# Turning x without its norm factor, in four transfers, with the factor applied to the first projection's sums

## Chip, cores, metric

One core of one Trainium2 chip. The metric is the device time of one launch in microseconds (us), the median over several runs. In the profile PE is the tensor engine's matmuls, PEld its weight loads, DVE the vector engine, ACT the scalar engine, SP the sync engine; a "q" behind a name (ACTq, SPq) is that engine's issuing of DMAs.

## What is computed

Two transformer blocks, one after the other, on one sequence of 256 tokens of width 2048, in float32. The change touches the very beginning of the first block, the RMS norm of the input and the projection that follows:

```python
def rmsnorm(x, g):
    y = xf * lax.rsqrt(jnp.mean(xf * xf, axis=-1, keepdims=True) + EPS)
    return (y * g.astype(jnp.float32)).astype(x.dtype)

h = rmsnorm(x, norm_mix[l])          # x: (1, 256, 2048)
z = h @ w_in[l]                      # w_in: (2048, 9472)
hq, hf, hi, hgate, aq, ak, av, g_hg, g_at = jnp.split(z, offsets, axis=-1)
```

The parts of `z` feed a gated linear recurrence (hq, hf, hi, hgate), a windowed attention (aq, ak, av; queries and keys are normed again per head) and two gates; then follow an output projection, a feed-forward part of width 8192, and a second block of similar shape.

## The kernel before

**Weights stream.** All weight matrices are cut into panels of 512 input features by 512 columns (1 MB), which SP loads into four slots of `raw`. A panel is two halves. For each half ACT writes its rounded high part to `wh` (`feed`, L1082) and DVE the remainder to `wl` (`feed`, L1782); both keep four halves ahead of PE at most, because `wh` and `wl` have four slots (`half_used`). PE makes of a half 4 tiles x (2 matmuls of `wh` with 512 columns, 2 of `wl` with 256): function `step`, L484 and L488. The 512 columns are the 256 tokens' high part and their low part, both in `hs`. Four panels (8 halves) are one step, which gives 512 columns of `z`; the first layer has 11 of them, numbered from 0 (two of them, for hi, run with the operands exchanged, function `across`).

**End of a step.** ACT copies the second half of each accumulator to `te` (`copy_halves`), DVE adds it to the first half and writes `z` (`total`, L1823), and signals `tile_summed`. A step may reuse its PSUM banks once the step before last is summed.

**The beginning.** x comes in two transfers of 128 tokens each, on SP's queue, ahead of the first panel. ACT squares and sums each (L1205), takes the root of both (L1211), DVE inverts it and multiplies x with it in four pieces of 512 features (`first_normed`, L1968, result `xn`). PE transposes `xn` (`first_turn(j)`, L618: 4 transposes for 256 features, j = 0 to 7), ACT scales the result by `norm_mix` and writes the high part (`first_high(j)`, L1218), DVE writes the low part (`first_low(j)`, L1976, signal `hs_lo`). Half h of step 0 needs `first_low(h)`. Turns 0 to 3 stand ahead of step 0, turns 4 to 7 behind its halves 0 to 3, and `vectors_turn`, which transposes small parameter vectors, behind half 5.

**Order.** Each engine runs its own list of instructions in the order in which the code writes it; semaphores link the lists. So a wait in ACT's list holds up all that stands behind it, its later `feed`s too.

**Two other places.** Queries are normed in step 10 (the last, 2 tiles wide): `pair_squares` on ACT waits until step 9 (z index 36 to 39) is fully summed, squares it into `psq` (L1185), and PE's `query_sums` (L593, behind half 3 of step 10) adds the squares up. In the feed-forward part the kernel already applies a norm factor behind a projection: it puts the factors on a diagonal (`turned_r`, L2299), spreads them over the partitions with a matmul by ones (`factors_across`, L546), copies them to `rstd` and multiplies the sums.

Of the kernel before, what the change touches and what calls it, by code (L numbers as in the profile page):

```python
# [23 lines left out]
P = 128  # L24
# [96 lines left out]
def build(nc, x, norm_mix, w_in, lb_logits, hg_norm, q_norm, k_norm, sinks, w_hg_out, w_at_out,  # L121
# [9 lines left out]
    with ctx:  # L131
# [136 lines left out]
        vectors_loaded, small_loaded, x_loaded = sem("vectors_loaded"), sem("small_loaded"), [sem("x_loaded0"), sem("x_loaded1")]  # L268
# [13 lines left out]
        def _(sp):  # L282
# [13 lines left out]
            for t in range(2):  # L296
                sp.dma_start(xin[:, t, :], x[0, t * P:(t + 1) * P, :]).then_inc(x_loaded[t], 16)
# [169 lines left out]
        def _(pe):  # L467
# [73 lines left out]
            def factors_across():  # L541

                pe.wait_ge(sem("row_diagonal"), 2)
# [67 lines left out]
            def first_turn(j):  # L611

                pe.wait_ge(sem("x_normed"), 2 * (j // 2) + 2)
                if j >= 4:
                    pe.wait_ge(sem("hs_lo"), 2 * (j - 4) + 2)
                for a in range(2):
                    for t in range(2):
                        mm = nc.tensor.transpose(ps[:, 4 + j % 4, a * T + t * P:a * T + (t + 1) * P],  # L618
                                                 xn[:, t, (2 * j + a) * P:(2 * j + a + 1) * P], ident[:])
# [5 lines left out]

            def vectors_turn():
                pe.wait_ge(vectors_loaded, 16 * N_VECTORS)
# [217 lines left out]
            def ffn_chunk(c):  # L845
                t = LF1.step + 4 * c
                for s in range(4):
# [4 lines left out]
                    if (c, s) == (0, 1):  # L852
                        pe.wait_ge(sem("rooted"), 1)
# [219 lines left out]
        def _(act):  # L1073
            def feed(h, dp):
# [4 lines left out]
                if q == 0:  # L1079
# [123 lines left out]
            for t in range(2):  # L1203
                act.wait_ge(x_loaded[t], 16)
                nc.scalar.activation(xn[:, t, :], xin[:, t, :], ACT.Square, accum_out=x_sum[:, t:t + 1]  # L1205
                                     ).then_inc(sem("x_squared"), 1)
                if t == 0:
                    act.wait_ge(sem("vectors_turned"), 1)
                    nc.scalar.activation(cols[:, 0:ND], ps[:, 3, 0:ND], ACT.Copy).then_inc(sem("cols_ready"), 1)
            act.wait_ge(sem("x_squared"), 2)  # L1210
            nc.scalar.activation(x_root, x_sum, ACT.Sqrt, bias=eps, scale=1.0 / D).then_inc(sem("x_rooted"), 1)  # L1211
# [56 lines left out]
            def hg_values(d):  # L1268

                for i in range(2):  # L1270
                    if i == 0:
                        act.wait_ge(across_done, d + 1)
                    else:
                        act.wait_ge(half_used, 8 * (5 + d) + 4)
                    nc.scalar.activation(z[:, Z_HI + 4 * d:Z_HI + 4 * d + 4, i * P:(i + 1) * P],
                                         ps[:, 4 * d + i, :].rearrange("p (h c) -> p h c", h=4), ACT.Copy
                                         ).then_inc(sem("v_ready"), 1)

            for d in range(2):
# [122 lines left out]
            def gates_out(s):  # L1402
# [3 lines left out]
                for i in range(2):  # L1406
# [4 lines left out]
                    nc.scalar.activation(gs[:, i, :], ps[:, (2, 0)[s % 2] + i, :], ACT.Copy  # L1411
# [49 lines left out]
            def hidden(c):  # L1461

                for s in range(4):
                    p, t = LF1.panel + 4 * s, LF1.step + 4 * c + s
                    for h in range(8):
                        feed(2 * p + h + 4, 32 * c)
                        if (c, s) == (0, 0):
# [5 lines left out]
                            if h == 5:  # L1473
                                act.wait_ge(sem("norm_summed"), 1)
# [291 lines left out]
        def _(dve):  # L1766
# [58 lines left out]

            def summed(t, dt, n):
# [135 lines left out]
            dve.wait_ge(sem("x_rooted"), 1)  # L1962
            link(nc.vector.reciprocal(x_root, x_root))

            def first_normed(q):
                c = slice(512 * q, 512 * q + 512)
                for t in range(2):
                    nc.vector.tensor_scalar(xn[:, t, c], xin[:, t, c], x_root[:, t:t + 1], None, ALU.mult  # L1968
                                            ).then_inc(sem("x_normed"), 1)
# [716 lines left out]
```

## Time and profile before

| what | value |
|---|---|
| median of 3 runs | 2529.32 us (2529.02 to 2529.37) |
| span of the profiled execution, first to last instruction | 2527.6 us |
| what lies around the span, against the median | 1.7 us |
| PE busy | 2493.5 us, 99% of the span |
| DVE busy | 1779.8 us, 70% |
| ACT busy | 1229.6 us, 49% |
| first matmul of step 0 | 15.73 us after the span's start |

The profiled execution's own time is not given apart from its span; the runs agree within 0.35 us, so span plus 1.7 us is taken for it. Busy shares are means over the whole span; what one place costs is read from the timeline around it. PE is busy almost always, so each microsecond in which it waits or does extra work counts nearly in full, and work of DVE or ACT counts only where PE is made to wait for it.

### The profile page before, as it was taken

The page shows a single profiled execution, that of the slowest core. Times are in us where ns is not written, and L with a number is a line of the kernel's source. Part 1 is how long each engine was busy: PE and PEld are TensorE (multiplying, and loading weights), DVE is VectorE, ACT ScalarE, POOL GpSimd, SP SyncE. Part 2 cuts the span into 40 slices and gives each one's busy share as a digit, 9 for nine tenths or more (in the row PEclk, how much of TensorE's full clock was granted, in tenths as well). Part 3 has the DMA queues.
Part 4 walks back from the last instruction along what each step waited for, and adds up shares of the span by engine and source line. Part 5 has one row for each costly group of instructions (what it writes and reads, how often), then busy time and mean ns, then how long its engine had stood idle before and what let it go on. Part 6 is the DMA issues. An engine that isn't in the chain of part 4 may idle for free.

```text
span 2527.6 us, 33151 instructions
## 1 busy us (share of the span) xinstructions
PE 2493.5 (99%) x13297; PEld 2116.8 (84%) x13297; DVE 1779.8 (70%) x2426; ACT 1229.6 (49%) x1801; POOL 0.2 (0%) x4
## 2 busy tenths in 40 slices
PE   8999999999999999999999999999899999999998
PEld 7888877888888888888887899978788888888887
DVE  6556657577788788788888767676866556665555
ACT  6456446454544444443444444565544444443453
POOL 0000000000000000000000000000000000000000
PEclk9999999999999999999999999999999999999999
DMA  7555445888778879879788545456577667657554
GB/s 260 192 186 180 153 146 179 300 294 280 264 263 302 283 268 317 283 261 327 261 281 297 180 160 169 143 166 215 177 239 236 221 212 234 226 190 214 186 183 134
DMA packets 324537, 572.53 MB, mean 227 GB/s; under 512 B 28649, under 2 KB 124215, under 8 KB 323487
## 3 DMA queue, kind: packets, MB, share of 16 engines
q1 hardware_dynamic: 277484, 449.44, 53.8%
q10 hardware_dynamic: 46899, 120.97, 13.7%
q8 instruction: 105, 1.72, 0.3%
q14 instruction: 49, 0.40, 0.0%
HBM read 560.63 MB, written 8.60 MB: 225 GB/s over the span
## 4 chain that ended last, share of the span: by engine, by line
PE 94%; DVE 3%; ACT 1%; DMA 1%; issue 1%; ACTq 0%; DVEq 0%; SPq 0%
PE ps L484 28%; PE ps L513 14%; PE ps L488 14%; PE ps L514 14%; PE ps L515 14%; PE ps L1002 2%; PE ps L1003 2%; PE ps L1004 2%; DVE wl L1782 1%; DMA gate_at<-gate_spill 1%; ACT wh L1082 1%; PE ps L888 1%; PE ps L593 0%; PE ps L687 0%; DVE ts L1906 0%
## 5 line engine op out<-in xcount | busy, mean ns | idle before, releaser
L1782 DVE TENSOR_TENSOR wl<-raw,wh 128x1024 fp32r<-128x1024 f32 x856 | 1041.0, 1223 | 710.1 <-ACT wh L1082 707.4
L1082 ACT ACTIVATE wh<-raw 128x1024 fp32r<-128x1024 f32 x856 | 899.4, 1058 | 1083.9 <-PE ps L515 505.3
L484 PE MATMUL ps<-hs,wh 128*128 128x512 f32 (+1 forms) x3152 | 994.6, 397 | 1.1 <-DVE hs L1854 0.7
L488 PEld LDWEIGHTS ps<-hs,wl 128*128 128x128 f32 (+1 forms) x3152 | 592.9, 188 | 141.2
L488 PE MATMUL ps<-hs,wl 128*128 128x256 f32 (+1 forms) x3152 | 620.7, 278 | 0.0
L484 PEld LDWEIGHTS ps<-hs,wh 128*128 128x128 f32 (+1 forms) x3152 | 481.9, 189 | 3.2 <-issue 1.5
L513 PE MATMUL ps<-wh,ff 128*128 128x512 f32 x864 | 336.2, 389 | 0.0
L514 PE MATMUL ps<-wl,ff 128*128 128x512 f32 x864 | 336.1, 389 | 0.0
L515 PE MATMUL ps<-wh,ff 128*128 128x512 f32 x864 | 336.1, 389 | 0.0
L513 PE MATMUL ps<-wh,hs 128*128 128x512 f32 x640 | 257.2, 402 | 0.0
L515 PE MATMUL ps<-wh,hs 128*128 128x512 f32 x640 | 249.8, 390 | 0.0
L514 PE MATMUL ps<-wl,hs 128*128 128x512 f32 x640 | 249.6, 390 | 0.0
L515 PEld LDWEIGHTS ps<-wh,ff 128*128 128x128 f32 x864 | 162.2, 188 | 33.7
L513 PEld LDWEIGHTS ps<-wh,ff 128*128 128x128 f32 x864 | 162.2, 188 | 33.5
L514 PEld LDWEIGHTS ps<-wl,ff 128*128 128x128 f32 x864 | 162.2, 188 | 33.1
L513 PEld LDWEIGHTS ps<-wh,hs 128*128 128x128 f32 x640 | 120.2, 188 | 30.1 <-issue 5.5
L515 PEld LDWEIGHTS ps<-wh,hs 128*128 128x128 f32 x640 | 120.1, 188 | 26.4
L514 PEld LDWEIGHTS ps<-wl,hs 128*128 128x128 f32 x640 | 120.4, 188 | 22.9
L1800 DVE SCALAR_TENSOR_TENSOR ada_acc<-ada_more,sm_cols,ada_acc 128x1024 f32<-128x1024 f32 x96 | 122.7, 1278 | 0.0
L1002 PE MATMUL ps<-hs,wh 128*128 128x256 f32 x384 | 111.0, 289 | 0.0
L1003 PE MATMUL ps<-hs,wl 128*128 128x256 f32 x384 | 108.6, 283 | 0.0
L1004 PE MATMUL ps<-hs,wh 128*128 128x256 f32 x384 | 108.5, 283 | 0.0
(296 smaller groups left out, 1782.7 us busy)
## 6 DMA issues: line engine op xcount, KB each, us to landing
raw<-w_in SPq DMA_DIRECT2D x112, 1024.0 KB
raw<-w_down SPq DMA_DIRECT2D x108, 1024.0 KB
raw<-w_up SPq DMA_DIRECT2D x64, 1024.0 KB
ada_w<-w_ada ACTq DMA_DIRECT2D x96, 512.0 KB, 5.5
ada_more<-w_ada ACTq DMA_DIRECT2D x96, 512.0 KB, 6.4
raw<-w_gate SPq DMA_DIRECT2D x88, 512.0 KB
raw<-w_up SPq DMA_DIRECT2D x88, 512.0 KB
raw<-w_out SPq DMA_DIRECT2D x16, 1024.0 KB
```

Source lines behind the costliest of these rows:

```text
L484: nc.tensor.matmul(ps[0:m, b, :], wh[:, slot, w0:w0 + m], rhs(n, k), start=k == 0, stop=False)
L488: mm = nc.tensor.matmul(ps[0:m, b, 0:T], wl[:, slot, w0:w0 + m], rhs(n, k)[:, 0:T], start=False, stop=k == 4 * panels - 1)
L513: nc.tensor.matmul(sums, hi, wh[:, slot, w], start=k == 0, stop=False)
L514: nc.tensor.matmul(sums, hi, wl[:, slot, w], start=False, stop=False)
L515: mm = nc.tensor.matmul(sums, lo, wh[:, slot, w], start=False, stop=k == 2 * last + 1)
L888: mm = nc.tensor.matmul(ps[:, 4 + i % 4, QT[qt]], z[half(i), Z_IQ + i // 2, qt * P:(qt + 1) * P], z[half(i), Z_IK, 0:KEYS[qt]], start=True ...
L1002: nc.tensor.matmul(sums, wh[:, slot, w0:w0 + m], hs[:, k, 0:T], start=k == 0, stop=False)
L1003: nc.tensor.matmul(sums, wl[:, slot, w0:w0 + m], hs[:, k, 0:T], start=False, stop=False)
L1004: mm = nc.tensor.matmul(sums, wh[:, slot, w0:w0 + m], hs[:, k, T:2 * T], start=False, stop=k == ND - 1)
L1082: nc.scalar.activation(wh[:, h % WH_SLOTS, :], raw[:, slot, HALF * q:HALF * (q + 1)], ACT.Copy).then_inc(wh_ready, 1)
L1782: nc.vector.tensor_tensor(wl[:, h % WH_SLOTS, :], raw[:, slot, HALF * q:HALF * (q + 1)], wh[:, h % WH_SLOTS, :], ALU.subtract).then_inc(wl ...
L1800: ins = nc.vector.scalar_tensor_tensor(out=ada_acc[:], in0=ada_ring[k % 4], scalar=csil[:, k:k + 1], in1=ada_acc[:], op0=ALU.mult, op1=ALU ...
```

## The change

- x's two transfers on SP's queue become four on ACT's queue, each of 512 features of all 256 tokens, so that `xin[p, t, d]` is token 128 t + p, as before. SP's queue begins with the first weight panel, which is cut into two transfers with a semaphore each.
- PE transposes x itself (`xin`), not `xn`; DVE's `first_normed` is gone. Turns 0 and 1 stand ahead of step 0, turns 2 to 7 behind its halves 0 to 5.
- The squares of x and their root stand in ACT's list behind the `feed`s at halves 4 and 5 of step 0. DVE inverts behind its `feed` at half 5 and writes the two diagonals; PE's new `factors_of_x` stands behind half 6, ahead of `vectors_turn`, which moved there from half 5; ACT copies the factors to `rstd` ahead of the parameter columns; step 1 waits for that.
- `total` becomes `totals_of_x` for every step of the first layer that writes `z` in this layout: the 4 sums as before, then 4 multiplies by `rstd`, and only these signal `tile_summed`. Where tokens lie on partitions (hi, gates) the factor is the `scale` of a copy that ACT makes anyway.

```diff
-            for t in range(2):
-                sp.dma_start(xin[:, t, :], x[0, t * P:(t + 1) * P, :]).then_inc(x_loaded[t], 16)
...
+                        if (i, s, k) == (0, 0, 0):
+                            sp.dma_start(slots[:, 0, 0:2, :], win[:, 0:2, 0:512]).then_inc(sem("first_loaded"), 16)
+                            sp.dma_start(slots[:, 0, 2:4, :], win[:, 2:4, 0:512]).then_inc(raw_loaded[0], PANEL_INC)
+                            continue
...
             def first_turn(j):
-                pe.wait_ge(sem("x_normed"), 2 * (j // 2) + 2)
+                pe.wait_ge(x_loaded[j // 2], 16)
...
+            def factors_of_x():
+                pe.wait_ge(sem("row_diagonal"), 2)
+                pe.wait_ge(sem("hs_lo"), 12)
+                for i in range(2):
+                    mm = nc.tensor.matmul(ps[:, 5, i * P:(i + 1) * P], ones[:], turned_r[:, i, :], start=True, stop=True)
+                mm.then_inc(sem("norm_summed"), 1)
...
-            for j in range(4):
-                first_turn(j)
+            first_turn(0)
+            first_turn(1)
             step(0, 0, 0, 0, FULL, from_hs, split=(sem("hs_lo"), 0),
-                 after=dict([(h, first_turn_after(4 + h)) for h in range(4)] + [(5, vectors_turn)]))
+                 after=dict([(h, first_turn_after(2 + h)) for h in range(6)] + [(6, vectors_turn)]))
             pe.wait_ge(sem("hs_lo"), ND)
             pe.wait_ge(sem("cols_ready"), 3)
+            pe.wait_ge(sem("rooted"), 1)
...
+            x_tokens = x[0].rearrange("(t p) d -> p t d", t=2)
+            for q in range(4):
+                act.dma_start(xin[:, :, 512 * q:512 * q + 512], x_tokens[:, :, 512 * q:512 * q + 512]
+                              ).then_inc(x_loaded[q], 16)
...
+            def x_square(t):
+                for q in range(4):
+                    act.wait_ge(x_loaded[q], 16)
                 nc.scalar.activation(xn[:, t, :], xin[:, t, :], ACT.Square, accum_out=x_sum[:, t:t + 1]
                                      ).then_inc(sem("x_squared"), 1)
+                if t:
+                    act.wait_ge(sem("x_squared"), 2)
+                    nc.scalar.activation(x_root, x_sum, ACT.Sqrt, bias=eps, scale=1.0 / D).then_inc(sem("x_rooted"), 1)
...
                     if s == 0 and h < 4:
                         first_high(4 + h)
+                    if s == 0 and h in (4, 5):
+                        x_square(h - 4)
                     if (s, h) == (0, 6):
+                        act.wait_ge(sem("norm_summed"), 1)
+                        nc.scalar.activation(rstd[:, 0, :], ps[:, 5, 0:T], ACT.Copy).then_inc(sem("rooted"), 1)
...
+            def totals_of_x(t, tiles):
+                for n, dst in enumerate(tiles):
+                    dve.wait_ge(half_copied, 4 * t + n + 1)
+                    nc.vector.tensor_tensor(dst, ps[:, bank(t, n), 0:T], te[:, n, :], ALU.add).then_inc(sem("dve_part"), 1)
+                if t == 0:
+                    dve.wait_ge(sem("rooted"), 1)
+                for n, dst in enumerate(tiles):
+                    dve.wait_ge(sem("dve_part"), 4 * t + n + 1)
+                    nc.vector.tensor_tensor(dst, dst, rstd[:, 0, :], ALU.mult
+                                            ).then_inc(tile_summed, 1 if n < len(tiles) - 1 else 4 - n)
...
+            def x_invert():
+                dve.wait_ge(sem("x_rooted"), 1)
+                nc.vector.reciprocal(x_root, x_root).then_inc(sem("x_rooted"), 1)
+                dve.wait_ge(sem("x_rooted"), 2)
+                for i in range(2):
+                    nc.vector.tensor_scalar(turned_r[:, i, :], ident[:], x_root[:, i:i + 1], None, ALU.mult
+                                            ).then_inc(sem("row_diagonal"), 1)
```

ACT's list before, from the end of its DMA issues to the first two halves (L1205 squares, L1211 root, L1082 `feed`, L1218 `first_high`):

```order
L1202 ACTIVATE sm_cols<-sm_cols 128x1 [waits consts_set]
L1205 ACTIVATE xn,sm_cols<-xin 128x2048 [waits x_loaded0]
L1209 ACTIVATE cols<-ps 128x16 [waits vectors_turned]
L1205 ACTIVATE xn,sm_cols<-xin 128x2048 [waits x_loaded1]
L1211 ACTIVATE sm_cols<-sm_cols 128x2 [waits x_squared]
L1082 ACTIVATE wh<-raw 128x1024 [waits half_used,raw_loaded0,cols_ready]
L1218 ACTIVATE hs<-ps,cols 128x256 [waits xn_turned]
```

ACT's list of the change, from the `feed` of half 7 on, which is where the squares (L1228) and the root (L1232) stand now; L1096 is `feed`, L1239 `first_high(7)`, L1272 the copy of the factors:

```order
L1096 ACTIVATE wh<-raw 128x1024 [waits half_used]
L1239 ACTIVATE hs<-ps,cols 128x256 [waits xn_turned]
L1239 ACTIVATE hs<-ps,cols 128x256
L1096 ACTIVATE wh<-raw 128x1024 [waits half_used,raw_loaded0]
L1228 ACTIVATE xn,sm_cols<-xin 128x2048 [waits x_loaded2,x_loaded3,x_loaded1,x_loaded0]
L1096 ACTIVATE wh<-raw 128x1024 [waits half_used]
L1228 ACTIVATE xn,sm_cols<-xin 128x2048 [waits x_loaded2,x_loaded3,x_loaded1,x_loaded0]
L1232 ACTIVATE sm_cols<-sm_cols 128x2 [waits x_squared]
L1096 ACTIVATE wh<-raw 128x1024 [waits half_used,raw_loaded1]
L1272 ACTIVATE rstd<-ps 128x256 [waits norm_summed]
```

So both squares and the root moved from ahead of the first `feed` to behind the `feed`s of halves 8 and 9, and those stand behind `first_high(7)`.

PE's list of the change, the end of half 6 and the beginning of half 7 of step 0; L633 is `factors_of_x`, L640 and L641 `vectors_turn`:

```order
L486 MATMUL ps<-hs,wh 128x512 x2
L490 MATMUL ps<-hs,wl 128x256 x2
L633 MATMUL ps<-turned_r,ones 128x128 [waits hs_lo,row_diagonal]
L633 MATMUL ps<-turned_r,ones 128x128
L640 MATMUL ps<-ident,rows_88 128x96 [waits hs_lo,vectors_loaded]
L641 MATMUL ps<-ident,rows_89 128x124
L486 MATMUL ps<-hs,wh 128x512 [waits wl_ready,hs_lo]
```

Before, nothing stood between halves 6 and 7; the two transposes of the vectors stood a half earlier, and there was no wait for a diagonal.

DVE's list of the change around the end of step 0; L1856 are the sums, L1861 the multiplies, L2006 the diagonals:

```order
L1808 TENSOR_TENSOR wl<-raw,wh 128x1024 [waits wh_ready] x2
L2003 RECIPROCAL sm_cols<-sm_cols 128x2 [waits x_rooted]
L2006 TENSOR_SCALAR turned_r<-ident,sm_cols 128x128 [waits x_rooted]
L2006 TENSOR_SCALAR turned_r<-ident,sm_cols 128x128
L1808 TENSOR_TENSOR wl<-raw,wh 128x1024 [waits wh_ready] x2
L1856 TENSOR_TENSOR z<-ps,te 128x256 [waits half_copied] x4
L1861 TENSOR_TENSOR z<-z,rstd 128x256 [waits dve_part,rooted]
L1861 TENSOR_TENSOR z<-z,rstd 128x256 [waits dve_part] x3
```

Before, the four sums (L1823) were followed by the next `feed` at once.

## Rows read from the trace of the kernel before

**Rows 1.** The page: busy time, and the chain that ended last

```profile
PE 2493.5 (99%) x13297; PEld 2116.8 (84%) x13297; DVE 1779.8 (70%) x2426; ACT 1229.6 (49%) x1801; POOL 0.2 (0%) x4
PE 94%; DVE 3%; ACT 1%; DMA 1%; issue 1%; ACTq 0%; DVEq 0%; SPq 0%
```

**Rows 2.** Timeline to step 0: start, duration, engine, line, operands [idle before]

```profile
8.90 1.91 ACT L1205 ACTIVATE xn<-xin 128x2048 f32<-128x2048 f32 x1 [0.45 <-DMA xin<-x]
10.94 0.29 ACT L1211 ACTIVATE sm_cols<-sm_cols 128x2 f32<-128x2 f32 x1
11.68 1.06 ACT L1082 ACTIVATE wh<-raw 128x1024 fp32r<-128x1024 f32 x1 [0.45 <-DMA raw<-w_in]
12.40 3.67 PE L618 MATMUL ps<-ident,xn 128*128 128x128 f32 x16 [5.07 <-DVE xn L1968]
13.55 0.84 ACT L1218 ACTIVATE hs<-ps,cols 128x256 fp32r<-128x256 f32 x2 [0.81 <-PE ps L618]
15.73 0.94 PE L484 MATMUL ps<-hs,wh 128*128 128x512 f32 x2
```

**Rows 3.** DMAs: xin's times to landing, ident's median, one window (last: GB/s)

```profile
DMA to landing us min/median/max: 5.6/6.7/7.7
...
ident<-k_ident ACTq DMA_DIRECT2D x1, 64.0 KB, 5.4
...
8.00:10.00 2.00, 0.00 (x0) 0.00 (x0) 0.00 (x0) 1.55 (x4) 0.00 (x0) 1.00 1.04 406
```

**Rows 4.** Timeline, PE: first matmuls of halves 3, 4 and 7 and of step 1

```profile
26.25 0.71 PE L484 MATMUL ps<-hs,wh 128*128 128x512 f32 x2
...
29.50 0.71 PE L484 MATMUL ps<-hs,wh 128*128 128x512 f32 x2
...
38.17 0.62 PE L484 MATMUL ps<-hs,wh 128*128 128x512 f32 x2
...
40.96 0.62 PE L484 MATMUL ps<-hs,wh 128*128 128x512 f32 x2
```

**Rows 5.** Timeline, ACT: two feeds with one first_high between

```profile
15.94 1.08 ACT L1082 ACTIVATE wh<-raw 128x1024 fp32r<-128x1024 f32 x1
...
16.89 0.85 ACT L1218 ACTIVATE hs<-ps,cols 128x256 fp32r<-128x256 f32 x2
...
17.60 1.09 ACT L1082 ACTIVATE wh<-raw 128x1024 fp32r<-128x1024 f32 x1
```

**Rows 6.** Timeline of the feed-forward part: root, spread by ones, next half

```profile
685.43 0.29 ACT L1138 ACTIVATE sm_cols<-sm_cols 128x2 f32<-128x2 f32 x1 [1.02 <-DVE sm_cols L1880]
...
686.50 0.71 PE L546 MATMUL ps<-turned_r,ones 128*128 128x128 f32 x4 [0.42 <-DVE turned_r L2299]
...
686.97 0.70 PE L484 MATMUL ps<-hs,wh 128*128 128x512 f32 x2
```

**Rows 7.** Windows (PE busy and count first, clock third last) and PE's idle times

```profile
38.00:60.00 22.00, 22.00 (x128) 19.21 (x127) 15.61 (x32) 15.25 (x23) 0.00 (x0) 1.00 0.60 198
...
1381.19 1.23 PE L569 MATMUL ps<-ident,a_rows 128*128 128x128 f32 x6 [2.59 <-DVE a_rows L1896]
...
1380.00:1390.00 10.00, 7.93 (x32) 6.38 (x33) 9.01 (x21) 4.62 (x9) 0.00 (x0) 0.66 0.54 178
...
1384.00:1388.00 4.00, 4.00 (x13) 3.43 (x14) 3.94 (x9) 2.61 (x5) 0.00 (x0) 0.50 0.17 63
...
1779.85 1.11 PE L569 MATMUL ps<-ident,f_rows 128*128 128x128 f32 x4 [6.09 <-DVE f_rows L1896]
...
1775.00:1789.00 14.00, 7.61 (x29) 5.86 (x30) 13.11 (x30) 8.57 (x22) 0.00 (x0) 0.63 0.09 23
```

**Rows 8.** Timeline around the sums of step 9 and the queries' squares

```profile
242.97 1.41 DVE L1823 TENSOR_TENSOR z<-ps,te 128x256 f32<-128x256 f32 x4
...
244.65 1.17 ACT L1185 ACTIVATE psq<-z 128x512 f32<-128x512 f32 x2
...
248.28 1.90 PE L593 MATMUL ps<-psq,sel 128*20 128x256 f32 x8 [0.17 <-ACT psq L1185]
```

More of the change, by code:

```diff
@@ L267, in build @@
         ada_spilled, ada_back = sem("ada_spilled"), sem("ada_back")
-        vectors_loaded, small_loaded, x_loaded = sem("vectors_loaded"), sem("small_loaded"), [sem("x_loaded0"), sem("x_loaded1")]
+        vectors_loaded, small_loaded, x_loaded = sem("vectors_loaded"), sem("small_loaded"), [sem(f"x_loaded{q}") for q in range(4)]
         block = ctx.enter_context(nc.Block())
@@ L618, in first_turn @@
                         mm = nc.tensor.transpose(ps[:, 4 + j % 4, a * T + t * P:a * T + (t + 1) * P],
-                                                 xn[:, t, (2 * j + a) * P:(2 * j + a + 1) * P], ident[:])
+                                                 xin[:, t, (2 * j + a) * P:(2 * j + a + 1) * P], ident[:])
                 mm.then_inc(sem("xn_turned"), 1)
@@ L624, in first_turn_after @@
                 return lambda: first_turn(j)
+            def factors_of_x():
[4 more added lines that the diff above has]
+                mm.then_inc(sem("norm_summed"), 1)
             def vectors_turn():
+                factors_of_x()
                 pe.wait_ge(vectors_loaded, 16 * N_VECTORS)
@@ L1078, in feed @@
                 slot, q = (h // 2) % RAW_SLOTS, h % 2
-                if q == 0:
+                if h == 0:
+                    act.wait_ge(sem("first_loaded"), 16)
+                elif q == 0 or h == 1:
                     act.wait_ge(raw_loaded[slot], PANEL_INC * (h // 8 + 1) + PANEL_INC // 4 * dp)
@@ L1199, in _ @@
                           ).then_inc(sem("ident_loaded"), 16)
+            x_tokens = x[0].rearrange("(t p) d -> p t d", t=2)
+            for q in range(4):
+                act.dma_start(xin[:, :, 512 * q:512 * q + 512], x_tokens[:, :, 512 * q:512 * q + 512]
+                              ).then_inc(x_loaded[q], 16)
             act.wait_ge(sem("consts_set"), 3)
             nc.scalar.activation(m8[:, 1, 4:5], eps, ACT.Sqrt)
-            for t in range(2):
-                act.wait_ge(x_loaded[t], 16)
+            act.wait_ge(sem("vectors_turned"), 1)
+            nc.scalar.activation(cols[:, 0:ND], ps[:, 3, 0:ND], ACT.Copy).then_inc(sem("cols_ready"), 1)
+            def x_square(t):
+                for q in range(4):
+                    act.wait_ge(x_loaded[q], 16)
                 nc.scalar.activation(xn[:, t, :], xin[:, t, :], ACT.Square, accum_out=x_sum[:, t:t + 1]
                                      ).then_inc(sem("x_squared"), 1)
[L1207 to L1211, printed above, removed]
+                if t:
+                    act.wait_ge(sem("x_squared"), 2)
+                    nc.scalar.activation(x_root, x_sum, ACT.Sqrt, bias=eps, scale=1.0 / D).then_inc(sem("x_rooted"), 1)
             def first_high(j):
@@ L1275, in hg_values @@
                     nc.scalar.activation(z[:, Z_HI + 4 * d:Z_HI + 4 * d + 4, i * P:(i + 1) * P],
-                                         ps[:, 4 * d + i, :].rearrange("p (h c) -> p h c", h=4), ACT.Copy
-                                         ).then_inc(sem("v_ready"), 1)
+                                         ps[:, 4 * d + i, :].rearrange("p (h c) -> p h c", h=4), ACT.Copy,
+                                         scale=x_root[:, i:i + 1]).then_inc(sem("v_ready"), 1)
+            act.wait_ge(sem("x_rooted"), 2)
             for d in range(2):
@@ L1410, in gates_out @@
                         act.wait_ge(half_used, 2 * (LG.panel + 4 * s) + 12)
-                    nc.scalar.activation(gs[:, i, :], ps[:, (2, 0)[s % 2] + i, :], ACT.Copy
+                    nc.scalar.activation(gs[:, i, :], ps[:, (2, 0)[s % 2] + i, :], ACT.Copy, scale=x_root[:, i:i + 1]
                                          ).then_inc(sem("gate_copied"), 1)
@@ L1960, in _ @@
             nc.vector.memset(m8[:, 1, 0:2], 0.0).then_inc(ada_folded, 1)
[L1962 to L1969, printed above, removed]
+            def x_invert():
[5 more added lines that the diff above has]
+                                            ).then_inc(sem("row_diagonal"), 1)
             def first_low(j):
@@ L2038, in to_z @@
             def to_z(i, s, t):
-                for n in range(4):
-                    total(t, 2 * i, n, z[:, 8 * i + 4 * s + n, :])
+                totals_of_x(t + 2 * i, [z[:, 8 * i + 4 * s + n, :] for n in range(4)])
             for s in range(2):
@@ L2046, in _ @@
                         first_low(4 + h)
+                    if (s, h) == (0, 5):
+                        x_invert()
                     if (s, h) == (1, 0):
@@ L2127, in _ @@
                 if s < 10:
-                    for n in range(4):
-                        total(s - 2, 0, n, z[:, 4 * s + n, :])
+                    totals_of_x(s - 2, [z[:, 4 * s + n, :] for n in range(4)])
             def hg_mask(h):
```

21 lines of the change are left out of this document (7 added, 14 removed).

## The prediction

> **What bounds the kernel now.** I read the page first: PE is busy 99% of the span, and 94% of the chain that ended last is PE [rows 1]. So a part of the change counts as far as it moves PE's list, and the whole of it lies within the first 260 us. Next the timeline of the beginning. PE's first real work waits for a chain: x lands, ACT squares it twice (1.91 us each), takes the root by 11.23, DVE multiplies x, and PE can turn it at 12.40, after an idle time of 5.07 us put down to DVE; ACT's high part follows at 13.55 and step 0 starts at 15.73 [rows 2]. From there PE keeps its own pace: halves 3 and 4 start 3.25 us apart with a turn between them, half 7 and step 1 2.79 us apart without one [rows 4]. So a half is 2.79, a turn on PE 0.46, and step 0 lasts 25.23 us (15.73 to 40.96). Later feeds and sums of ACT and DVE lie beside that.
>
> **Term 1: the start.** Gone from the path are the squares, the root and DVE's multiplies. What starts the chain now is the landing of x's first quarter. To time it I fit the transfers of before: 2.1 MB of x and the small ones landed at 8.9 us, when ACT's second wait for x ended [rows 2] (5.6 to 7.7 us after their issue [rows 3]), and panel 0, 3.2 MB in all, at 11.68, when ACT's feed of half 0 stopped waiting for it [rows 2]. The rate was some 0.4 MB per us (406 GB/s in one window [rows 3]), which makes a landing 3.5 us plus bytes over 0.395. x's first quarter (0.52 MB) stands in ACT's queue behind ident and norm_mix, 0.07 MB; SP's queue is about 0.9 us ahead (0.36 MB), and then I let both queues have half the rate each: 0.36 + 2 x 0.6 = 1.56 MB, so 7.4 us. The two queues did share before: ident, 64 KB, took 5.4 us beside x [rows 3]. From a turn's start to ACT's high part was 1.15 us (12.40 to 13.55), from there to step 0 2.18 (13.55 to 15.73) [rows 2]. Step 0 starts at 7.4 + 1.15 + 2.18 = 10.7, and **5.0 us are won**. The first panel's first half (0.52 MB, in front of its queue) lands earlier than x's quarter, and the high parts of ACT need no more than one feed (1.06) ahead. Bounds: if the quarter had the whole rate, it would land at 5.0 and the start be 8.3, if ACT is through with its issues by then; if SP's first two panels' worth went ahead of it, (2.1 + 0.6)/0.395 + 3.5 = 10.3, start 13.6. I take 10.7, since the row of ident shows sharing. Panel 1 and x's later quarters land by the same rule at 13.2 and 10 to 15.5; they are wanted from 14 to 24, so I cost them at nothing, and about 1 us of delay each if the cover is short.
>
> The Trainium skill (DMA: Bandwidth & Descriptors, Queues, rings and completion order) has each DMA engine take turns between the queues that hold work, which is the half rate that the row of ident suggests; by that rule alone the start is again 10.7.
>
> **Term 2: work that moves onto PE's list.** Two of the four turns that stood ahead of step 0 now stand inside it, 2 x 0.46 = 0.9 us. The factors' two matmuls by ones cost 0.47, as in the feed-forward part (686.50 to 686.97 [rows 6]). `vectors_turn` only moves by a half. **1.4 us lost.**
>
> **Term 3: a hole in step 0.** This is what I think matters most. PE waits behind half 6 for the diagonal. Turn 7 now stands behind half 5, so ACT's `first_high(7)` waits for it, and in ACT's list the feed of half 8, the first square, the feed of half 9, the second square and the root all stand behind `first_high(7)`. Counted from the end of half 5 on PE: turn 7 and its signal 0.85 (an estimate between the 0.46 that a turn takes on PE and the 1.15 of a cold one), a high pair 0.71 (16.89 to 17.60), a feed 0.95 (15.94 to 16.89 [rows 5]), a square 1.91, a feed 0.95, a square up to the root's start 2.04 (8.90 to 10.94 [rows 2]), the root 0.29, then reciprocal, two diagonals and the signal to PE 0.78 (685.72 to 686.50 [rows 6]). The sum is 8.5 us. PE meanwhile has turn 7 and half 6, 3.25 us. **PE stands still for 5.2 us.** The feeds of halves 8 and 9 don't rescue it: they are needed only by step 1, but they are in the list. Nor is their panel late: its load waits for DVE's second feed and for SP's small transfers, as before. Bounds: 4.5 (0.3 less at the turn, less at the squares) and 6.5 (panel 4 late by 1.3). Step 1's new wait for `rstd` costs nothing: after the root ACT has one feed (0.95) and the copy of the factors, while PE runs half 7, 2.79 us; without this cover it would cost about 0.5.
>
> Step 0 then takes 8 x 2.79 for its halves, 6 x 0.46 for turns, 5.2 for the hole, 0.47 for the factors and 0.3 for the vectors' transposes (29.50 to 38.17 is 8.67, 3 halves and 0.3 [rows 4]): 31.1 us. Started at 10.7 it ends at 41.8, against 40.96 before: **the start's gain is used up, +0.8 us.** (The sum of the terms, -5.0 + 1.4 + 5.2, is 1.6; the other 0.8 is PE's stalls between the first halves before, when DVE's late multiplies of x held up turn 4: 25.23 is that much longer than 8 x 2.79 + 4 x 0.46 + 0.3.)
>
> **Term 4: the clock behind the hole.** In the trace PE's granted clock falls from 2.4 to 1.2 GHz at the two places in mid-kernel where PE had stood idle: 2.59 us before 1381.19, where the mean of ten us was 0.66, thus 6.8 us at the lower level; and 6.09 us before 1779.85, with 0.63 over 14 us, 10.4 us at the lower level. In 1384 to 1388, wholly at the lower level, PE started 13 matmuls in 4 us (3.25 per us), against 128 in 22 us (5.8 per us) at the full one [rows 7]: a stretch of dense matmuls loses 0.44 of its length. A hole of 5.2 us lies between these two. I let 1.8 of the 6.8 us fall into the hole and 5 on dense matmuls: **2.2 us lost**. Bounds: nothing, since the idle 5.07 us before 12.40 drew no lower level (step 0's first pair took 0.94 us), and 3.6 (8 us, from the longer case).
>
> The Trainium skill (TensorE: Matmul & The Clock Gate, Part 1) says that idleness brings the array to 1.2 GHz and activity releases it; by it the sum holds Term 4, without it the sum is that of the first rival. The same section calls the lower rate the default before any activity, and there the trace disagrees, as step 0 began at the full pace.
>
> **Term 5: the multiplies on DVE.** Each step of the first layer gets 4 multiplies 128x256, about as dear as the 4 sums (1.41 us for four [rows 8]). In steps 0 to 8 they are hidden: PE has four halves of cover (11 us), and DVE was busy for 15.61 of the 22 us of a step [rows 7]. Behind step 9 they are not. The squares of the queries start at 244.65, 0.3 us after the sums end (244.38) [rows 8]; now they wait for the multiplies, to 245.85, 1.2 us later. PE's `query_sums` is already held up there by these squares (idle 0.17 at 248.28 [rows 8]). Through two squares, two feeds (0.95 each) and the next two squares, PE is done with them at 251.5 instead of 250.18: **1.3 us lost**. Bounds 0.9, and 1.8 if the two multiplies behind step 10 also delay the next feed.
>
> **Nothing:** the scales in ACT's copies for hi and the gates (a Copy with a scale, as `first_high` is one already), and the renamed semaphores.
>
> **Sum.** 0.8 + 2.2 + 1.3 = 4.3 us over the profiled execution: span 2527.6 to 2531.9. With the 1.7 us around it that is, against the median, 2529.3 + 4.3 = 2533.6. A change of 0.2%, 5.1 us, is about what measurement can tell from none; so I forecast no change that can be told, on the slow side.
>
> **Rivals.**
> - *The same without the lower clock.* For it speaks the idle time ahead of 12.40; against it both idle times in mid-kernel. 0.8 + 1.3 = +2.1: 2531.4.
> - *x's first quarter is late.* It starts behind SP's panels instead of beside them, ACT's four issues taking long or the queue being served second. The start is 13.6 and not 10.7, +2.9 on everything: +7.2, 2536.5, slower. It decides from a landing 0.8 us later than I forecast. The shared rate before speaks against it, the many small descriptors of x in its new form for it. A low clock of 8 us, 0.8 + 3.6 + 1.3 = +5.7, 2535.0, ends on the same side.
> - *No hole.* ACT gets to the squares early enough, so that Terms 3 and 4 fall away: 0.8 - 5.2 + 1.3 = -3.1: 2526.2. ACT's list speaks against it, since `first_high(7)` stands ahead of the squares. Even so the gain stays under 0.2%.
>
> **Chances.** Forecast 0.47, no lower clock 0.23, late x or a long low clock 0.22, no hole 0.08. The range takes in the first three: from -0.3 (no lower clock, start 8.3 in place of 10.7) to +7.9 (late x, 0.7 for the other bounds): 2529.0 to 2537.2. The likeliest case alone spans 2531.6 to 2535.4. Slower by over 0.2%: nearly all of the third and a quarter of the first, 0.33. Faster by over 0.2%: 0.03. Within: 0.64.
>
> **What the profile will show.** Step 0 starts near 10.7 (Term 1); an idle time of PE of about 5.2 us put down to DVE's diagonals, with `factors_of_x` behind it near 38 (Term 3); granted clock below 1.0 in 36 to 45 (Term 4); step 1 near 42 at full clock or 44 with the lower one; PE's wait at the queries' squares grown by over 1 us near 250 (Term 5). I am wrong if step 0 starts after 12, if PE doesn't wait behind half 6, or if the steps after the first run at another pace than 2.79 us a half because DVE's added work reaches PE.

## The result and the profile after

The changed kernel takes 2537.52 us (6 runs, 2536.63 to 2539.08) where the kernel before takes 2529.17 (6 runs): ratio 1.0034, 95% interval 1.0023 to 1.0044. It is slower by 8.4 us, 0.34%, twice what I forecast and 0.3 us outside my range. The profiled execution spans 2536.2 us, 8.6 more than before.

PE's idle times by releaser (us in total, times, longest), changed kernel:

```profile
PE ps L645 <- DMA rows<-norm_mix: 5.4, 1, 5.4
PE ps L633 <- DVE turned_r L2006: 4.8, 1, 4.8
PE ps L620 <- DMA xin<-x: 3.9, 1, 3.9
...
PE ps L595 <- ACT psq L1199: 1.2, 2, 1.0
```

The wait for `xn` is gone, and two that did not exist stand in its place: 3.9 us for x, and 4.8 us for the diagonals. The beginning, in the timeline of the changed kernel, answers to [rows 2] and [rows 4]:

```profile
1.73 2.40 ACTq L1216 DMA_DIRECT2D xin<-x  x4
...
5.93 1.06 ACT L1096 ACTIVATE wh<-raw 128x1024 fp32r<-128x1024 f32 x1
...
9.58 1.97 PE L620 MATMUL ps<-ident,xin 128*128 128x128 f32 x8 [3.90 <-DMA xin<-x]
...
12.58 1.19 PE L486 MATMUL ps<-hs,wh 128*128 128x512 f32 x2 [1.03 <-issue]
...
14.00 1.05 PE L486 MATMUL ps<-hs,wh 128*128 128x512 f32 x2
15.28 1.05 PE L486 MATMUL ps<-hs,wh 128*128 128x512 f32 x2
16.56 1.05 PE L486 MATMUL ps<-hs,wh 128*128 128x512 f32 x2
...
18.55 0.79 PE L486 MATMUL ps<-hs,wh 128*128 128x512 f32 x2
19.41 0.62 PE L486 MATMUL ps<-hs,wh 128*128 128x512 f32 x2
```

Step 0 starts 3.15 us earlier than before, not 5.0. And its first half goes at 1.28 us per tile (14.00, 15.28, 16.56) where later ones go at 0.70: half 1 starts 5.97 us after half 0, against 3.25 for a half with a turn. That is 2.7 us which the forecast had at nothing. The pace changes near 18.7 us, and there the trace has its first entry of the granted clock, at 1.00 (18.72). (The trace holds these entries, each with its start, length and level; the views print only means made of them.) Then the hole, ACT and DVE ahead of it and the clock behind it:

```profile
35.11 0.84 ACT L1239 ACTIVATE hs<-ps,cols 128x256 fp32r<-128x256 f32 x2 [1.46 <-PE ps L620]
...
36.79 1.91 ACT L1228 ACTIVATE xn<-xin 128x2048 f32<-128x2048 f32 x1
...
38.68 1.05 ACT L1096 ACTIVATE wh<-raw 128x1024 fp32r<-128x1024 f32 x1
39.63 1.90 ACT L1228 ACTIVATE xn<-xin 128x2048 f32<-128x2048 f32 x1
...
41.65 0.29 ACT L1232 ACTIVATE sm_cols<-sm_cols 128x2 f32<-128x2 f32 x1
...
42.18 0.48 DVE L2006 TENSOR_SCALAR turned_r<-ident,sm_cols 128x128 f32<-128x128 f32 x2
...
42.72 1.22 PE L633 MATMUL ps<-turned_r,ones 128*128 128x128 f32 x4 [4.84 <-DVE turned_r L2006]
...
43.97 1.20 PE L486 MATMUL ps<-hs,wh 128*128 128x512 f32 x2
...
45.39 0.92 PE L486 MATMUL ps<-hs,wh 128*128 128x512 f32 x2
...
47.79 0.63 PE L486 MATMUL ps<-hs,wh 128*128 128x512 f32 x2
```

ACT is never idle from 35.11 to the root at 41.65, and PE is idle 4.84 us. From the factors at 42.72 to step 1 at 47.79 PE takes 5.07 us, where 0.47 + 0.3 + 2.79 = 3.56 would do at the full clock. The windows of the changed kernel (third last: granted clock) show the clock there:

```profile
38.00:42.00 4.00, 0.00 (x0) 0.00 (x0) 1.40 (x3) 3.97 (x7) 0.00 (x0) 1.00 0.33 129
42.00:44.00 2.00, 1.28 (x7) 1.28 (x7) 1.70 (x4) 0.92 (x2) 0.00 (x0) 0.65 0.83 239
44.00:46.00 2.00, 2.00 (x8) 1.71 (x7) 0.15 (x1) 0.75 (x3) 0.00 (x0) 0.50 0.94 351
```

The trace's entries of the granted clock put the lower level (1.2 GHz) at 42.62 to 46.03. The first tile of half 7 takes 1.42 us there (43.97 to 45.39), exactly what the first tile of half 0 took (12.58 to 14.00): half 0 ran at the pace of the lower level.

The 1.5 us are the cheapest case. In the profiles of experiments 2, 3, 4 and 10, with a hole of the same 4.8 us, the lower level lasted 6.8 us and began inside the hole, and the way from the factors to step 1 took 5.39, 5.92, 6.10 and 6.27 us in place of 3.56: 1.8 to 2.7 us lost.

At the queries, where [rows 8] show 0.17 us of idle time:

```profile
251.14 1.42 DVE L1861 TENSOR_TENSOR z<-z,rstd 128x256 f32<-128x256 f32 x4
...
252.59 1.15 ACT L1199 ACTIVATE psq<-z 128x512 f32<-128x512 f32 x2 [0.97 <-DVE z L1861]
...
256.21 1.90 PE L595 MATMUL ps<-psq,sel 128*20 128x256 f32 x8 [0.95 <-ACT psq L1199]
```

The pieces, in us:

| piece | forecast | measured, against before |
|---|---|---|
| start of step 0 | -5.0 | -3.15 |
| half 0 at the lower pace | 0 | +2.7 |
| turns and factors on PE's list | +1.4 | +1.4 |
| hole behind half 6 | +5.2 | +4.84 |
| clock behind the hole | +2.2 | +1.5 |
| stalls of before that go | -0.8 | -0.8 |
| start of step 1 | +3.0 | +6.83 (the pieces give 6.5) |
| queries' squares | +1.3 | +1.1 |
| the rest of the span | 0 | +0.7 |

### The profile page after: what moved, and what is told of

It reads as the page before. It is cut to its first block, busy times and chain, and to the rows that moved or that the text cites. A ratio compares the mean times of both kernels' runs of the same rounds, so it can differ in the third digit from the quotient of the medians.

```text
span 2536.2 us, 33198 instructions
## 1 busy us (share of the span) xinstructions
PE 2498.1 (98%) x13301; PEld 2120.2 (84%) x13301; DVE 1789.1 (71%) x2454; ACT 1232.4 (49%) x1802; POOL 0.2 (0%) x4
## 4 chain that ended last, share of the span: by engine, by line
PE 94%; DVE 2%; ACT 1%; DMA 1%; issue 1%; ACTq 0%; DVEq 0%
PE ps L486 28%; PE ps L490 14%; PE ps L515 14%; PE ps L517 14%; PE ps L516 14%; PE ps L1014 2%; PE ps L1015 2%; PE ps L1016 2%; DMA gate_at<-gate_spill 1%; DVE wl L1808 1%; ACT wh L1096 1%; PE ps L900 1%; PE ps L595 0%; PE ps L699 0%; DVE ts L1944 0%
## 5 line engine op out<-in xcount | busy, mean ns | idle before, releaser
L1096 ACT ACTIVATE wh<-raw 128x1024 fp32r<-128x1024 f32 x856 | 899.7, 1058 | 1075.0 <-PE ps L517 503.3
```

The costliest lines, as they stand in the source:

```text
L1096: nc.scalar.activation(wh[:, h % WH_SLOTS, :], raw[:, slot, HALF * q:HALF * (q + 1)], ACT.Copy).then_inc(wh_ready, 1)
```

## The experiments

All are built on the changed kernel, except where it says otherwise. Medians; ratios are against the kernel before, run on the same chip beside them (2528.9 to 2529.1). The changed kernel's own 2537.5 is from its own set of runs, so differences to it are good to about half a microsecond at best.

**1. Squares earlier.**

```diff
-                    if s == 0 and h in (4, 5):
-                        x_square(h - 4)
+                    if s == 0 and h in (0, 2):
+                        x_square(h // 2)
...
-                    if (s, h) == (0, 5):
+                    if (s, h) == (0, 3):
                         x_invert()
```

> The changed kernel with ACT's two squares of x moved ahead, behind first_high(4) and first_high(6), and DVE's inversion behind its feed of half 7; PE's factors stay behind half 6. Theory A (the wait of PE behind half 6 comes from where the squares stand in ACT's list): PE's idle of 4.84 us there goes, and with it the lower clock behind it (5.07 us from the factors to step 1 where 3.56 would do, so 1.5 us); some 0.5 to 1 us comes back because first_high(5) and (7) are a little late. 2537.5 - 6.3 + 0.8 = 2532.0, between 2531.2 and 2533. Rival B (the squares' 4 us on ACT cost PE wherever they stand inside step 0): the stall only moves to the high parts, 2535 or more.

Measured 2530.54, ratio 1.0005 (0.9996 to 1.0015): 7.0 us of the 8.4 gone, 0.7 below theory A's range. In this kernel's timeline the hole is 0.69 us, and the squares run in ACT's idle time between high parts:

```profile
25.26 1.92 ACT L1228 ACTIVATE xn<-xin 128x2048 f32<-128x2048 f32 x1
...
31.74 1.91 ACT L1228 ACTIVATE xn<-xin 128x2048 f32<-128x2048 f32 x1
...
37.71 0.71 PE L633 MATMUL ps<-turned_r,ones 128*128 128x128 f32 x4 [0.69 <-DVE turned_r L2006]
```

The granted clock is 1.00 there, and the factors' matmuls take 0.71 us in this row in place of 1.22. So it is the place in ACT's list, not the squares' 4 us. I had allowed 0.8 us for late high parts; they were not late. Part of the gain is not the squares': half 0 and its turn took 5.23 us in this execution and 5.97 in the changed kernel's.

**2. PE warmed ahead of step 0.**

```diff
+            for _ in range(9):
+                nc.tensor.transpose(ps[:, 2, 0:P], ident[:], ident[:])
             first_turn(0)
             first_turn(1)
+            for _ in range(3):
+                nc.tensor.transpose(ps[:, 2, 0:P], ident[:], ident[:])
```

> The changed kernel with 9 extra transposes of ident on PE while it waits for x and 3 more between turn 1 and step 0 (results unused). Theory A (half 0 ran at 1.28 us per tile in place of 0.70 because PE came to it at the lower clock, which before was hidden by 16 transposes in a row): half 0 now runs at 0.70 per tile, 2.3 us are won, 2535.2 (2534.7 to 2536); the wait behind half 6 stays at 4.8. Rival B (half 0 is slow because its operands or the DMA traffic hold it up): its tiles stay at 1.28 and the time at 2537.5 or above.

Measured 2535.1, ratio 1.0024 (1.0014 to 1.0033), 2.4 us less than the changed kernel, with the hole at 4.84 as before. Half 0 of this kernel:

```profile
12.79 1.19 PE L486 MATMUL ps<-hs,wh 128*128 128x512 f32 x2 [0.39 <-issue]
...
14.08 0.63 PE L486 MATMUL ps<-hs,wh 128*128 128x512 f32 x2
...
14.78 0.63 PE L486 MATMUL ps<-hs,wh 128*128 128x512 f32 x2
```

Step 0 starts 0.2 us later, with the same operands and DMA traffic, and from the second tile on it goes at 0.70 us. The trace's first entry of the clock stands at 13.90 here, between those two tiles. What PE did just before decides, and not its operands: rival B falls.

**3. No factor for the queries.** `totals_of_x` for steps 8 and 9 makes the four sums alone, and they signal `tile_summed`. The multiplies by `rstd` are left out there.

```diff
+                if t in (6, 7):
+                    for n, dst in enumerate(tiles):
+                        total(t, 0, n, dst)
+                    return
...
```

> The changed kernel without the four multiplies by rstd behind steps 8 and 9 (the queries, which are normed per head afterwards, so the factor all but cancels; this part of the computation is left out). Theory A (the multiplies cost only where ACT's squares of the queries wait for them): PE's idle at the queries' sums falls from 1.21 back to 0.2, 1.1 us are won, 2536.4 (2535.9 to 2537). Rival B (the multiplies cost nothing there): 2537.5. Rival C (the 34 multiplies press on DVE in each step): more than 2 us are won and steps 2 to 7 shorten.

Measured 2536.02, ratio 1.0028 (1.0017 to 1.0039), 1.5 us less (runs from 2534.64 to 2537.45). PE's idle time at the squares is 0.17 us again. This is theory A; the squares' wait explains 1.1 us, and the other 0.4 lie within that spread. C is out by the changed kernel's own timeline: from the start of step 1 to the end of `query_sums` it takes 210.3 us (47.79 to 258.11), the kernel before 209.2 (40.96 to 250.18), and those 1.1 us are all at the squares.

**4. The arithmetic alone**, with x's two transfers and the first panel on SP's queue as before.

```diff
...
+            for t in range(2):
+                sp.dma_start(xin[:, t, :], x[0, t * P:(t + 1) * P, :]).then_inc(x_loaded[t], 16)
...
-                pe.wait_ge(x_loaded[j // 2], 16)
+                for t in range(2):
+                    pe.wait_ge(x_loaded[t], 16)
...
```

> Only the arithmetic part of the change: x in two transfers ahead of the first panel on SP's queue as before, the panel in one piece, all else as in the changed kernel. Theory A: the first turn can start at 8.9 us, but the feed of half 0 waits for panel 0 until 11.7 as before and stands ahead of first_high(0) in ACT's list, so step 0 starts near 14.5 and not 12.6; with the wait and the clock as in the changed kernel that is 2539.4 (2538.5 to 2540.5). Rival B (the four small transfers are what makes the changed kernel slow): 2535 or less.

Measured 2538.97, ratio 1.0039 (1.0024 to 1.0054). PE turns x at 8.70 but starts step 0 at 14.54, after 3.90 us idle, since `first_high(0)` stands behind a feed that waits for panel 0. The arithmetic alone wins only 1.2 us at the start; it needs the early half panel to win more.

**5. The transfers alone**, on the kernel before.

> Only the other part of the change: the kernel before with x in four transfers on ACT's queue and the first panel in two; the arithmetic as before, so ACT's squares wait for all of x. Theory A (x's bytes share the rate with the panels; the last quarter lands near 16.1 in place of 8.9): the squares begin 7.3 us later and step 0 starts near 23, 2536.2 (2535 to 2537.5). Rival B (transfers are hidden anyway): 2529.

Measured 2540.83, ratio 1.0046 (1.0032 to 1.006). The direction is theory A's, the size is not: I was 4.6 us short. ACT's first square in this kernel:

```profile
18.06 1.91 ACT L1215 ACTIVATE xn<-xin 128x2048 f32<-128x2048 f32 x1 [12.52 <-DMA xin<-x]
```

The last quarter is there at 18.06, not 16.1: I had counted its landing time from the first quarter's issue. And both squares now stand behind it (18.06 and 20.04), where in the kernel before the first ran from 6.38, while the rest of x was still on its way; I had left out that square too, 1.9 us. Step 0 then starts at 26.60, 10.9 us later than before, and the time grew by 11.9. Step 0 runs at 0.70 us per tile at once in it, right behind 16 transposes in a row.

**6. The hole filled** with 18 transposes of ident; PE still waits for the diagonal.

```diff
+                pe.wait_ge(sem("hs_lo"), 12)
+                for _ in range(18):
+                    nc.tensor.transpose(ps[:, 5, 0:P], ident[:], ident[:])
                 factors_of_x()
```

> The changed kernel with 18 transposes of ident on PE (results unused) inside the wait behind half 6, about 4.3 of its 4.8 us; the wait for the diagonal itself stays. Theory A (the wait also costs 1.5 us behind it, because the granted clock falls): the clock stays at 1.00 after 40 us, 2537.5 - 1.5 = 2536.0. Rival B (the lower clock there costs nothing that counts): 2537.5 or above.

Measured 2536.25, ratio 1.0027 (1.0016 to 1.0037), with runs from 2533.5 to 2539.2, too wide to settle 1.3 us by the time alone. In the one execution that was profiled (2534.95) the transposes took 2.13 us and not 4.3, an idle time of 2.88 us was left, and behind it the clock stayed at 1.00; the factors to step 1 took 3.55 us and not 5.07. So in this execution the 1.5 us were the clock's. That the filling works in every execution is not shown.

```profile
42.12 0.71 PE L633 MATMUL ps<-turned_r,ones 128*128 128x128 f32 x4 [2.88 <-DVE turned_r L2009]
```

**7. The three mends together** (1, 2 and 3).

> The changed kernel with the squares moved ahead (as in the first experiment), the warming transposes (second) and without the queries' multiplies (third) together. Theory A (the three losses are separate and the start's gain is then left over): 2530.5 - 2.3 - 1.3 = 2526.9 (2526.2 to 2527.8), faster than the kernel before by 2 us. Rival B (with PE at full speed in half 0, ACT's list is late by the squares, and the first gain is lost again): 2529.

Measured 2528.16, ratio 0.9996 (0.9987 to 1.0005): between the two theories. The timeline gives one reason. In this kernel's profile (of its slowest run, 2529.44) half 0 was slow again (tiles at 12.73, 14.15, 15.43; the trace's first entry of the clock at 16.36), though PE's list up to there is that of experiment 2, where the entry stood at 13.90. Twelve transposes with an idle time of some 2 us among them brought the full clock by the second tile in the one execution and by the fourth in the other.

**8. The same with the start filled**, 17 and 6 transposes in place of 9 and 3.

> The kernel with three mends, with 17 in place of 9 warming transposes ahead of turn 0 and 6 in place of 3 behind turn 1, so that PE is never idle for 2 us before step 0. In the profile of the kernel with 9 and 3 half 0 still took 4.5 us in place of 2.8. Theory A (those idle times kept the clock low in part of the runs): half 0 at 0.70 per tile throughout, 2528.2 - 1.3 = 2526.9. Rival B (the lower clock at the start has nothing to do with what PE does before): 2528.2.

Measured 2527.35, ratio 0.9992 (0.9983 to 1.0001), 0.8 us less than experiment 7. Half 0 of this kernel runs at the full pace from its first tile:

```profile
12.35 0.70 PE L486 MATMUL ps<-hs,wh 128*128 128x512 f32 x2 [0.80 <-issue]
...
13.13 0.62 PE L486 MATMUL ps<-hs,wh 128*128 128x512 f32 x2
```

The pace is theory A's: the trace's first entry of the clock stands at 8.95, inside the warming transposes. The times are not settled, as those of 7 and 8 overlap (2527.29 to 2529.44, 2526.51 to 2528.87). The profiled execution was the slowest of its ten, for another reason: PE lost 1.28 us in the first block, where it waits 0.08 us in the kernel before.

```profile
PE ps L829 <- DVE mixed_rows L2319: 1.3, 1, 1.3
```

**9. The kernel before with two turns ahead of step 0 in place of four**, all else as it was.

```diff
-            for j in range(4):
+            for j in range(2):
                 first_turn(j)
...
-                 after=dict([(h, first_turn_after(4 + h)) for h in range(4)] + [(5, vectors_turn)]))
+                 after=dict([(h, first_turn_after(2 + h)) for h in range(6)] + [(6, vectors_turn)]))
```

> The kernel before with only two of the four turns ahead of step 0 and the other six behind halves 0 to 5, all else as before. Theory A (the turns ahead of step 0 ran while PE waited anyway and brought it to the full clock; taking two away costs 0.9 us on the path and leaves half 0 at the lower clock for 1.5 to 2.5 us more): 2531.8 (2531.0 to 2532.6). Rival B (only the 0.9 us of the two turns count): 2529.8.

Measured 2531.09, ratio 1.0006 (0.9997 to 1.0015), by the medians 1.9 us over the kernel before and inside theory A's range; but the interval reaches 1, and in the profile, of its fastest run, step 1 starts at 42.04, only 1.1 us later than before. So the time does not decide between the theories. The pace does. Its half 0 has two and a half tiles at the lower pace:

```profile
15.15 1.19 PE L484 MATMUL ps<-hs,wh 128*128 128x512 f32 x2 [1.03 <-DVE hs L1976]
...
16.57 1.06 PE L484 MATMUL ps<-hs,wh 128*128 128x512 f32 x2
...
17.85 0.94 PE L484 MATMUL ps<-hs,wh 128*128 128x512 f32 x2
```

So a slow half 0 needs neither x's new transfers nor the moved norm. It comes with the order of the turns. It costs little here, since step 0 also starts 0.6 us earlier, and the kernel before had a slow first tile and a stall of its own in half 0.

**10. x's quarters among the panels on SP's queue**, no mends: quarter 0, first half panel, quarter 1, second half panel, panel 1, quarter 2, panel 2, quarter 3, panel 3.

> The changed kernel with x's quarters on SP's queue among the first panels, and nothing else changed (no mends). Theory A (the late landing of the first quarter, 9.6 us, came from its place beside the panels): the first quarter lands before 6.5, step 0 starts near 9.8 to 10.5, at the lower clock as in the changed kernel, and the wait behind half 6 stays at 4.8: 2537.5 - 2.5 = 2535.0 (2534.2 to 2536). Rival B (the earlier start is lost to the longer stretch at the lower clock): 2537.5.

Measured 2534.27, ratio 1.0021 (1.0012 to 1.003), 3.3 us less. The same quarter, of the same 2 KB rows, takes 4.6 us to land and not 7.8, and PE's first turn no longer waits for it. Step 0 starts at 10.20, at 1.28 us per tile. First the changed kernel's landing times, then this kernel's, and the start of its step 0:

```profile
DMA to landing us min/median/max: 7.8/11.3/14.4
```

```profile
DMA to landing us min/median/max: 4.6/8.5/13.2
...
10.20 1.19 PE L496 MATMUL ps<-hs,wh 128*128 128x512 f32 x2 [1.56 <-DVE hs L2020]
```

**11. This order with the three mends.**

> The kernel with the three mends, and x's quarters back on SP's queue, interleaved with the first panels: quarter 0, first half panel, quarter 1, second half panel, panel 1, quarter 2, panel 2, quarter 3, panel 3. Theory A (a quarter that stands first has the whole rate and lands near 5.5 in place of 9.6; then the warming transposes, which end near 7.7, and the first feed bind): step 0 starts near 11, 2525.4 (2524.5 to 2526.3). Rival B (a quarter's transfer is slow by its form, 256 pieces of 2 KB, in whichever queue): 2527.

Measured 2525.91 (11 runs, 2525.23 to 2527.18), ratio 0.9987 (0.9978 to 0.9996). **It beats both kernels**: 3.1 us, 0.13%, under the one before. The queries' factor is left out as in 3, so it computes a little less than they do. Its step 0:

```profile
11.05 0.70 PE L496 MATMUL ps<-hs,wh 128*128 128x512 f32 x2 [0.95 <-issue]
```

**12. The same without the warming transposes.**

> The kernel with x among the panels and the mends of the squares and of the queries, but without the 12 warming transposes. Theory A (they delay turn 0 from about 6.5 to 8.1 but save the lower clock): step 0 starts near 10, half 0 takes 5 us, 2525.9 - 1.2 + 2.3 = 2527.0. Rival B (the transposes only delay the start): 2524.7.

Measured 2526.78 (11 runs, 2526.58 to 2528.11), ratio 0.999 (0.9981 to 0.9999). Step 0 starts at 9.94 and not 11.05, but its half 0 takes 4.66 us, with tiles at 9.94, 11.36 and 12.64, where experiment 11 has 2.86. In the profiles the warming costs 1.1 us of start and gives 1.8 back; the medians differ by 0.9 us, and the two intervals overlap.

## Why the prediction was wrong

Two steps failed: the landing of x's first quarter (Term 1) was put 2.2 us too early, which cost 1.9 us at the start of step 0, and half 0's slow pace, 2.7 us, was not in the sum. By the sum neither alone would have left the range; together they put 4.6 us on it. The stated sign of error, step 0 after 12, came (12.58). That the time lies only 0.3 us outside the range is in part luck, as the hole, the clock behind it and the queries came out 1.3 us cheaper than forecast.

**Term 1 was mis-sized.** I had x's first quarter land at 7.4 us; it landed near 9.5, and PE turned it at 9.58. Once x moves, the two queues share the rate as I said: 0.34 MB on ACT's queue (q10) and 0.35 on SP's (q1) in 6 to 8 us. But in 4 to 6 us ACT's queue moved next to nothing. Changed kernel, DMA by queue in 4 to 6 and in 6 to 8 us:

```profile
q1 hardware_dynamic: 395, 0.75, 97.1%
q10 hardware_dynamic: 60, 0.06, 8.3%
...
q10 hardware_dynamic: 167, 0.34, 50.7%
q1 hardware_dynamic: 170, 0.35, 49.2%
```

SP's panels had the whole rate for 2 us more than the head start of 0.9 us, 0.36 MB, that I gave them. By the times of single packets, x, issued from 1.73, moves its first one at 5.62, when SP's queue has moved 1.07 MB; in the seven other profiled kernels with x on ACT's queue it is 5.35 to 5.67 and 0.98 to 1.10 MB. That is about the first panel (1.05 MB), the only part of the panels issued before x. Whether x waited for it was not tested, so why x moves so late stays open; experiment 10 shows only that in SP's queue, at its head, the same quarter does not suffer it. This was the rival of the late quarter in its mechanism, and with 1.9 us of delay (it decided from 0.8) alone enough to leave the band of no change.

**A cost was missing, and it is the larger failure.** Of Term 4 the prediction said that the idle time before 12.40 "drew no lower level", and of the rate that the Trainium skill gives for the time before any activity that "the trace disagrees, as step 0 began at the full pace". Both were misread. In [rows 2] the four turns at 12.40, 16 transposes, fill 3.67 us of PE right ahead of step 0, 0.23 us each, where later a turn, four transposes, takes 0.46 (0.12 each): they ran at the lower pace, and so did the first tile of step 0 (its pair 0.94 us against 0.62). PE had time for them, as it waited for DVE and ACT anyway, and they took the slow stretch upon themselves. The trace's first entry of the clock stands at 16.24 there. The change leaves 8 of these transposes (1.97 us) and an idle time of 1.03 us there, so that half 0 pays. Experiments 2, 9 and 12 show it from three sides: turns taken from the kernel before slow its half 0; transposes added to the changed kernel speed it up; taken away from the mended kernel, half 0 is slow again. The Trainium skill (TensorE: Matmul & The Clock Gate, Part 1) says that the low rate is the state before any activity; the first half's pace agrees, 1.28 us against 0.70, in every profile here in which few matmuls stand ahead of step 0. It costs 2.7 us in the changed kernel's profile, and 1.5 to 2.1 in those of experiments 1, 3, 10 and 12.

**Term 2** held: the turns, the factors and the vectors take what their rows said. The 0.8 us that the sum took for DVE's late multiplies were only in part a stall (0.38 us of idle time); some 0.3 were the slow first tile (1.01 us against 0.70).

**Term 3** was right in mechanism and size, 4.84 for 5.2. The 0.85 us for turn 7 and its signal was 0.63 (34.48 to 35.11). Experiment 1 is its proof.

**Term 4**, the clock behind the hole, came as forecast, but at 1.5 in place of 2.2 us in this profile. It fell later than I assumed, at 42.62, so that only 3.4 us were at the lower level. The 1.8 to 2.7 us of the four other profiles with this hole lie around the forecast.

**Term 5** was right: 1.1 for 1.3, and the multiplies cost PE nothing in the steps before (experiment 3).

What is left is 0.7 us: 0.2 between the queries and the second block's start (1381.19 before, 1389.35 after, a difference of 8.16) and 0.5 up to its feed-forward part (1779.85 and 1788.53, 8.68). Of the first, PE's wait for `mixed_rows`, 0.33 us against 0.08, is the whole. The second arises behind 1381, where both kernels have 6.83 us at the lower clock: it begins 1.15 us later in PE's list than before (1390.88 against 1381.57, with all else 8.16 us later) and so covers more dense matmuls. Both differ from one execution to the next.

The sum over experiments fits roughly: squares 7.0 (the hole 4.15, its clock 1.5, and 0.7 of half 0 in the two profiles), warming 2.4, queries 1.5. Added up they are 10.9, more than the 9.4 which experiment 7 shows. The half 0 that was slow again in it, 1.2 us longer than in experiment 2, can account for most of the missing 1.5; experiment 8, which filled the start, got 0.8 of it back.

## What to carry to other kernels

When work is taken off the head of the critical path, look at what else ran there for free: here 16 transposes brought PE to its full pace while it waited, and a few matmuls on data at hand (experiment 11) buy that back. Work that is moved "into the shadow" lands in one engine's list; count what stands ahead of it there, up to the instruction that it has to serve, since a wait is set by the list and not by the engine's mean load of 49%. And a transfer that the start depends on goes at the head of the queue that carries the bulk, not onto another queue beside it.

## What the runs showed of the hardware

The granted clock in the profile is no guide to the first microseconds. It reads 1.00 in both of these windows, of the changed kernel in half 0 and of the kernel before in half 0:

```profile
12.00:18.00 6.00, 5.42 (x17) 4.67 (x18) 3.63 (x6) 2.19 (x4) 0.00 (x0) 1.00 1.05 394
```

```profile
15.70:18.70 3.00, 3.00 (x17) 2.62 (x16) 3.00 (x5) 3.00 (x7) 0.00 (x0) 1.00 1.06 380
```

The 16 matmuls of half 0 and one transpose in each take 5.42 us of PE's time in the one and 3.00 in the other. The pace of the matmuls told, not the column. The reason lies in the trace: its entries of the clock begin only at 18.72 in the changed kernel and at 16.24 in the kernel before, and a window ahead of the first entry prints 1.00. In every kernel here this first entry, always 1.00, stands where the pace of PE's matmuls changes: from 8.95 us (experiment 8) to 26.34 (experiment 5).

The stretch at the lower pace also ends at different times in kernels with the same list up to there: half 0 and its turn took 5.97 us in the changed kernel, 5.23 in experiment 1, 4.77 in experiment 3. Behind the hole of 4.8 us, too, the lower level lasted 3.4 us in one profile and 6.8 in four, and it did not come behind idle times of 0.69 us (experiment 1) and of 2.88 us right behind 18 transposes (experiment 6). Some of the scatter of single times of the kernels here may come from this; it was not tested by itself.
